# Gated-delta core: decay rows of both lanes first, the 32-wide diagonal blocks straight from PSUM, the full score blocks made between the small levels

## The reference

```
G      = cumsum(g);  decay[i,j] = exp(G_i - G_j) for j <= i
a      = strict_lower( (beta_i k_i . k_j) * decay )
u, w   = (I + a)^-1 [ beta v , beta k exp(G) ]
intra  = (q . k) * decay
v_new  = u - w S;   o = (q exp(G)) S + intra v_new
S'     = S exp(G_last) + (k exp(G_last - G))^T v_new
```

## Time and profile before

| | us |
|---|---|
| median of 3 runs | 2628.5 |
| lowest, highest of them | 2626.69, 2628.72 |
| the profiled execution, its time | 2633.75 |
| its span, first to last instruction | 2631.2 |
| PE busy in the span | 2090.2 (79%) |
| DVE busy in the span | 789.9 (30%) |
| mean granted TensorE clock | 0.902 |

### The profile page before, as it was taken

How to read it: one execution, slowest core, us unless ns; L and a number is a source line. 1 busy time by engine, 2 the same in 40 slices (tenths; PEclk the granted TensorE clock), 3 DMA queues, 4 the chain that set the end, 5 groups by cost and what they waited for, 6 DMA issues and landing times.

```text
span 2631.2 us, 33285 instructions
## 1 busy us (share of the span) xinstructions
PE 2090.2 (79%) x13800; PEld 1370.7 (52%) x13800; DVE 789.9 (30%) x1509; ACT 541.4 (21%) x946; POOL 31.6 (1%) x49
## 2 busy tenths in 40 slices
PE   7877668998988997999886666665999977666665
PEld 6656445886755885777542222222777742222221
DVE  4543453566554574122220000002122130000002
ACT  3221133441124442042110000001033110000000
POOL 0000000000000000000000000000000000000000
PEclk9978879998998998999978888887999978888887
DMA  8200013765954675432339999999332419999997
GB/s 299 99 1 34 2 65 128 255 251 175 378 207 160 227 266 174 145 128 97 160 125 426 427 426 427 425 427 383 130 128 72 184 73 427 426 426 427 427 426 293
DMA packets 150294, 641.69 MB, mean 244 GB/s; under 512 B 9310, under 2 KB 30840, under 8 KB 117046
## 3 DMA queue, kind: packets, MB, share of 16 engines
q1 hardware_dynamic: 143898, 637.13, 61.1%
q10 hardware_dynamic: 6300, 3.20, 0.4%
HBM read 639.21 MB, written 1.10 MB: 243 GB/s over the span
## 4 chain that ended last, share of the span: by engine, by line
PE 57%; DMA 30%; DVE 6%; issue 3%; ACT 2%; DVEq 1%; POOL 1%; SPq 0%; ACTq 0%; POOLq 0%
DMA ring<-in_w_down 30%; PE psum L1149 6%; PE psum L807 5%; PE psum L808 5%; PE psum L809 5%; PE psum L1265 3%; PE psum L1063 3%; PE psum L785 3%; PE psum L1052 3%; PE psum L905 2%; PE psum L599 2%; PE psum L1142 2%; PE psum L1225 1%; PE psum L630 1%; PE psum L922 1%
## 5 line engine op out<-in xcount | busy, mean ns | idle before, releaser
L1245 PE MATMUL psum<-ring,arena 128*32 128x256 f32 x4096 | 295.0, 439 | 188.1 <-DMA ring<-in_w_up 146.4
L1245 PEld LDWEIGHTS psum<-ring,arena 128*32 128x32 f32 x4096 | 141.6, 122 | 344.2 <-issue 146.1
L1265 PE MATMUL psum<-ring,arena 128*32 128x512 f32 x1024 | 164.8, 776 | 93.6 <-DMA ring<-in_w_down 84.4
L807 PE MATMUL psum<-arena_r 128*128 128x512 f32 x512 | 208.0, 406 | 14.7 <-DVE h_featmajor_r L1319 7.6
L809 PE MATMUL psum<-ring_r,arena_r 128*128 128x512 f32 x512 | 205.3, 401 | 0.0
L1904 DVE TENSOR_TENSOR arena<-psum,arena 128x256 f32<-128x256 f32 x32 | 13.6, 425 | 564.0 <-PE psum L1245 564.0
L1149 PE MATMUL psum<-h_featmajor,ring 128*128 128x256 f32 x768 | 173.6, 379 | 0.0
L1345 DVE TENSOR_TENSOR ring_r<-ring,arena_r 128x2048 fp32r<-128x2048 f32 x64 | 143.7, 2286 | 86.2 <-ACT arena_r L1962 86.1
L1149 PEld LDWEIGHTS psum<-h_featmajor,ring 128*128 128x128 f32 x768 | 145.9, 190 | 19.9
L2282 ACT ACT_TABLE_LOAD x32 | 41.1, 1283 | 523.0 <-PE psum L1245 523.0
L1962 ACT CAST arena_r<-ring 128x2048 fp32r<-128x2048 f32 x64 | 119.6, 1904 | 71.1 <-PE psum L809 71.1
(11 more groups left out here) (358 smaller groups left out, 2595.6 us busy)
## 6 DMA issues: line engine op xcount, KB each, us to landing
ring<-in_w_gate SPq DMA_DIRECT2D x64, 2048.0 KB, 26.6
ring<-in_w_up SPq DMA_DIRECT2D x64, 2048.0 KB, 26.2
ring<-in_w_down SPq DMA_DIRECT2D x64, 2048.0 KB, 26.3
ring<-in_mlp_w SPq DMA_DIRECT2D x32, 2048.0 KB, 7.9
ring<-in_w_mod SPq DMA_DIRECT2D x24, 2048.0 KB, 11.5
ring<-in_w_in SPq DMA_DIRECT2D x20, 2048.0 KB, 8.2
ring<-in_gdn_w_in SPq DMA_DIRECT2D x8, 2048.0 KB, 17.8
ring<-in_dswa_w_in SPq DMA_DIRECT2D x9, 1536.0 KB, 14.9
```

Of the source, the lines that this page charges most:

```text
L807: mm(o, xh, wh, start=start, stop=False, skip_group_check=True)
L1245: ins = mm(PS[32 * j:32 * j + 32, 4 + m, 0:T], XGE[:, 4 * u + kk, :], W(v + 2 * m + u, D)[:, kk, j * T:(j + 1) * T], start=u == 0 and kk = ...
L1265: ins = mm(PS[32 * j:32 * j + 32, (7, 4)[half], :], HTE[:, k % 2, 32 * (k // 2):32 * (k // 2) + 32], W(v + 4 + u, D)[:, j, half * 512:(hal ...
```

## The change

- PE set-up: the rows of G of both lanes are made first, each followed by its own signal; after them, for each lane, the rows of beta and the score products. `core_setup` is raised four times a pass in place of twice. The matmuls are the same in number and shape.
- DVE set-up: the first two signals release L1471; the last two release the rest of a lane. The diagonal blocks AN are no longer copied out of KD: for each group of 32 partitions one multiplication reads the scores in PSUM and DT, and after a drain a second one multiplies by -1 and by the beta rows in PSUM.
- The full blocks: the two halves of the score product (`kd_raw`) and the multiplication by -beta (`kd_beta`) are moved behind `t_ready`: lane 0's upper half straight after the set-up (it is what reads bank 3, and signals `kd_half`), the rest after the small levels 0, 1 and 2.
- PE small levels: at level 0 PE waits for `kd_half` before `gate_step`, which writes bank 3. The product Q goes to columns 128 to 255 of bank 4l in place of bank 4l+1, so that the beta rows stay until `kd_beta` has read them.

```diff
                 for l in range(2):
                     for h in range(4):
                         g = d * 8 + hg + h
-                        mm(pair(4 * l, P)[:, h], GS[:, l, g:g + 1].to_broadcast([P, P]), CUM[:, d, :], start=True, stop=True)
+                        ins = mm(pair(4 * l, P)[:, h], GS[:, l, g:g + 1].to_broadcast([P, P]), CUM[:, d, :], start=True, stop=True)
+                    ins.then_inc(sem("core_setup"), 1)
+                for l in range(2):
...
+                    if q == 0:
+                        pe.wait_ge(sem("kd_half"), it + 1)
                     gate_step(it, q)
...
-                                ins = mm(PS[r, 4 * l + 1, h * Q32:(h + 1) * Q32], small[l]["U"][r, h], small[l]["PP"][r, h],
+                                ins = mm(PS[r, 4 * l, P + h * Q32:P + (h + 1) * Q32], small[l]["U"][r, h], small[l]["PP"][r, h],
...
+                def kd_raw(l, half):
+                    kd, dt = lanes[l]["KD"], lanes[l]["DT"]
+                    return v.tensor_tensor(kd[:, half:half + 2], PS[:, 4 * l + 2 + half // 2, :].rearrange("p (a b c) -> p a b c", a=2, b=2),
+                                           dt[:, half:half + 2].unsqueeze(2).to_broadcast([P, 2, 2, P]), ALU.mult)
+                def kd_beta(l):
+                    kd = lanes[l]["KD"]
+                    settle()
+                    v.scalar_tensor_tensor(kd[:, :, 0], kd[:, :, 0], -1.0, pair(4 * l + 1, P), ALU.mult, ALU.mult)
                 for l in range(2):
-                    dve.wait_ge(sem("core_setup"), 2 * it + l + 1)
+                    dve.wait_ge(sem("core_setup"), 4 * it + l + 1)
...
                 for l in range(2):
+                    dve.wait_ge(sem("core_setup"), 4 * it + l + 3)
                     dve.wait_ge(sem("dt_out"), 2 * it + l + 1)
-                    kd, dt = lanes[l]["KD"], lanes[l]["DT"]
-                    for half in (0, 2):
-                        v.tensor_tensor(kd[:, half:half + 2], PS[:, 4 * l + 2 + half // 2, :].rearrange("p (a b c) -> p a b c", a=2, b=2),
-                                        dt[:, half:half + 2].unsqueeze(2).to_broadcast([P, 2, 2, P]), ALU.mult)
+                    sm, dt = small[l], lanes[l]["DT"]
+                    for r in quads:
+                        qk = PS[r, 4 * l + 2:4 * l + 4, :].rearrange("p a (b c k) -> p (a b) c k", b=2, c=2)
+                        v.tensor_tensor(sm["AN"][r], qk[:, :, 0, r], dt[r, :, r], ALU.mult)
                     settle()
-                    v.scalar_tensor_tensor(kd[:, :, 0], kd[:, :, 0], -1.0, pair(4 * l + 1, P), ALU.mult, ALU.mult)
-                    settle()
-                    sm = small[l]
                     for r in quads:
-                        v.tensor_copy(sm["AN"][r], kd[r, :, 0, r])
+                        v.scalar_tensor_tensor(sm["AN"][r], sm["AN"][r], -1.0, pair(4 * l + 1, P)[r, :, r], ALU.mult, ALU.mult)
                     settle()
...
+                kd_raw(0, 2).then_inc(sem("kd_half"), 1)
                 v.tensor_tensor(R1, V[:, hs, fst, :], bc(BT[:, fst, d * 8 + hg:d * 8 + hg + 4], P), ALU.mult).then_inc(sem("r1_ready"), 1)
...
+                    if q == 0:
+                        kd_raw(0, 0)
+                    elif q == 1:
+                        kd_beta(0)
+                        kd_raw(1, 0)
+                    elif q == 2:
+                        kd_raw(1, 2)
+                        kd_beta(1)
```

More of the change, by code:

```diff
@@ L1497, in _ @@
                         v.copy_predicated(sm["Tm"], bm(masks32[:, d, q + 1], 4),
-                                          PS[:, 4 * l + 1, 0:P].rearrange("p (h c) -> p h c", c=Q32)).then_inc(sem("t_grown"), 1)
+                                          PS[:, 4 * l, P:2 * P].rearrange("p (h c) -> p h c", c=Q32)).then_inc(sem("t_grown"), 1)
                         settle()
                         v.transpose(sm["U"].rearrange("p h c -> p (h c)"), sm["Tm"].rearrange("p h c -> p (h c)")).then_inc(sem("u_grown"), 1)
+                    if q == 0:
[6 more added lines that the diff above has]
+                        kd_beta(1)
                 settle()
```

## The result

The changed kernel takes 2609.4 us (median of 4 runs, 2608.05 to 2610.09) against 2627.6 (2626.18 to 2628.72) of the kernel before: ratio 0.993, 95% interval 0.9915 to 0.9946. It is 18.2 us faster; 20 were forecast, 2608.5 us. The profiled execution took 2610.09 us, its span 2608.2. Two executions among the experiments, one of e2 (3217.6 us) and one of e4 (2947.8), ran in a slow state at a mean granted clock of 0.63 and 0.71 and stand in no ratio.

What follows compares the result with a forecast made beforehand. Passes bound by PE-DVE hand-overs, not by a full engine or memory. 4.97 - 0.15 = 4.8 us a pass, 19.3 in four, +1 for the clock, sum 20: 2628.5 - 20 = 2608.5 us, range 2600 to 2616.

Steps and rivals of the forecast that it cites:

- The set-up: Start of each pass on PE and DVE: lane 1's transposition ends at 209.74 in place of 214.71, 4.97 us less.
- The instruction that the trace did not show: DVE's diagonal blocks: a 32-partition instruction reading PSUM, taken at 0.30 us, four at 1.21 us without overlap.
- By overlaps: DVE's diagonal blocks: had instructions overlapped as L1471, twelve overlaps of 0.08 a pass, 3.8 us in all, sum 23, not 19.
- The new wait: PE's level 0 gate step waits for the half that reads bank 3: 0.1 to 0.2 us, taken as 0.15.
- The full blocks between the levels: Small levels on DVE: 1.41 us of moved work fits into an idle of 1.62, costed at nothing.
- The clock: Level 0 gate step: half clock still in about three passes of four; a full one gains 1.0; +1 us in all.
- The rival of dear strided reads: DVE's diagonal blocks: 0.69 us per 32-partition PSUM read makes the kernel 6 us slower, 2634; chance 0.05.
- that of an end that doesn't feel it: Behind the passes: passes shrink, but a later stretch absorbs it if a weight load set its start, 2628; chance 0.04.
- The one of the moved work: Between small levels: moved work sticks out 3.5 us a pass, leaving 5 us gain in all, 2623; chance 0.07.
- A clock kept full at the gate steps: Gate steps of level 0 and the level after at full clock: 1.3 us more a pass, some 7 more, 2601; chance 0.14.
- Its second half: Behind the small levels, at L716: the clock's drop, 3.48 us in the third pass, 2.10 in the fourth, may go too.

Runs made afterwards that it cites:

- e2: Changed kernel with PE's old order and old signals, so diagonal blocks from PSUM and moved full blocks alone: 2626.6 us, ratio 0.9983 to the kernel before.
- e4: Changed kernel with ten idle 128x128 products on PE between lane 0's and lane 1's products P at level 0: 2609.7 us, ratio 0.9923.
- e1: Kernel before with PE's new order and the two extra signals alone, full blocks still ahead of the diagonal copies: 2609.3 us, ratio 0.992.
- e3: Changed kernel with all full blocks straight behind the diagonal blocks, ahead of level 0, none between the levels: 2616.2 us, ratio 0.9948.
- e7: Changed kernel with two more half blocks, 0.65 us each, behind level 1 and behind level 2: 2618.6 us, ratio 0.996.
- e5: The changed kernel itself run again, with the kernel before on the same chip: 2608.2 us, ratio 0.992.
- e10: Changed kernel with the gate step of level 3 moved from between P and Q to behind Q: 2604.7 us, ratio 0.9888.
- e6: Changed kernel with bank 3's half block made between the lanes, level 0's gate step and lane 0's Q before lane 1's P: 2600.8 us, ratio 0.9896.
- e8: e4 with small products P and Q made for two of four 32-wide blocks only, output not valid: 2606.0 us, ratio 0.9912.

## Why the prediction was right

*The set-up.* Forecast 11.17 us from the first matmul to ready, measured 11.15 to 11.16 in passes two to four. e1 and e2 split it into 3.93 for the order and 1.06 for the blocks, which add up to the 4.99 measured. DVE took up lane 0's scores 4.71 us into the pass, as forecast (203.28 - 198.57). The sum has a slip: four instructions of 0.30 with three gaps of 0.013 are 1.24 us and not 1.21, so that ready would have been 11.29. The true 1.19 hid it.

*The instruction that the trace did not show.* Taken at 0.30, measured 0.287 and 0.284. Four took 1.19 us, 0.30 from one to the next, so without overlap. The Trainium skill ("VectorE: DVE Perf Modes", section "Two Vector instructions with no wait between them") says that a held instruction, here one whose operands begin in another group of 32 partitions, starts only when every earlier one has finished; the trace agrees. By overlaps the sum would have been 4 us too large.

*The new wait.* 0.15 taken. PE's weight loads stand idle 0.21 to 0.38 us for it. What it costs is less: where the gate step runs at the half clock, the first merge comes 3.50 us behind ready in place of 3.36, which is 0.14.

*The full blocks between the levels.* Costed at nothing; the least idle before lane 0's merge that remained was 0.24 us, 0.2 had been counted. Level 2 at the full clock lasts 2.91 us in both kernels. e3 shows the cover and e7 its edge.

*The clock* is the term that was off, in both directions. At the gate step of level 0 it stayed full, or nearly, in two passes of four (one of four in e5's profile); I had counted one. But the gate step of level 1, full before in three passes, ran at the half clock in part in all four, and so did the first wide product, in four in place of two. These rows of the fourth pass stand against 1.12 us and 2.10 us:

```profile
311.25 1.54 PE L630 MATMUL psum<-ring,h_featmajor 128*128 128x512 f32 x2
321.43 3.02 PE L720 MATMUL psum<-arena 128*128 128x128 f32 x16 [2.13 <-DVE arena L1528]
```

Against +1 us expected, the sections behind ready lost 2.3. The first pass gave 6.3 at the set-up, where the forecast had it like the others; the 1.4 us more came from the clock in the profile of the kernel before. Together the passes gave 19.0 of the 20, and the medians of the two kernels differ by 18.2. The mechanism and the set-up's size are shown; that the total came so close is in part luck, since these two terms of the clock offset each other in part, and the interval of the ratio allows 14 to 22 us.

*The rivals.* The rival of dear strided reads is refuted by 0.285 us, that of an end that doesn't feel it by the 20.2 us at the end of the first block. The one of the moved work is refuted for this amount; e7 shows where it begins. A clock kept full at the gate steps does not give its 7 us: in e4 the holes in the instruction supply took it back. Its second half, a clock that stays full behind the small levels too, was not there in e4 (full in one pass of four) and shows in e10.

## What to carry to other kernels

When two engines hand over to each other, look at what the waiting instruction reads, not at what its semaphore covers: a signal after the early product, with that product made first, gave 3.9 of 5.0 us a pass with no work removed. Work that must leave a path is best put where the trace shows a wait of known length, and that length is a budget, 1.62 us here, which 1.41 fit and 2.9 did not. A standstill of PE in one place and a long filler instruction on its path in another belong together (e6, e10).

## What was not expected of the hardware

PE ran out of instructions: with 256 records of 32x32 products a level (128 matmuls and as many weight loads) and the full clock, it stood up to 1.2 us in the middle of a product in e4 and 2.0 in e10, and with half of the records never (e8). What the half clock cost in these levels was in part a wait that PE would have had for its instructions anyway: in e4 5.1 us won at the gate steps came back as 5.1 us of holes.

The granted clock fell and rose at other places in each kernel, so that equal sections of a pass differ by 1.4 to 3 us: the rows of G took 1.86 us of loading, and 3.23 in e1's fourth pass at the half clock. With this the order of two kernels a few microseconds apart can't be told from one profile of each.
